# Folding a Fourier transform by residue, and moving the first output weights and the conv channel sums, in a hybrid trunk step

## What is computed

```python
hmix = rms_norm(x, norm_mix) * (1 + sc1) + sh1
q, k, v, conv_in, pool_in, four_in = split(hmix @ w_in)        # 2816 columns
attn = gqa_attention(rope(norm(q)), [cached keys, rope(norm(k))], ...)   # 8 heads of 64, 2 key heads
conv = silu(layer_norm(depthwise_conv31(a * sigmoid(gate))))   # 512 channels, norm over channels
pool = multi_scale_pool(pool_in) @ pool_w * pool_scale
four = fft2(four_in.reshape(L, 4, 128), axes=(0, 2)).real      # 4 groups, over tokens and channels
x = x + g1 * (concat([attn, conv, pool, four]) @ w_out)        # 2048 rows, 1024 columns
x = x + g2 * hier_moe(rms_norm(x) * (1 + sc2) + sh2)           # 16 experts, top 2 in one of 4 groups
y = rms_norm(x, final_norm)
```

## Time and profile before

| what | value |
|---|---|
| median of 3 runs (lowest, highest) | 703.83 us (702.86, 706.41) |
| the profiled execution: its own time | 707.6 us |
| its span, first to last instruction | 705.2 us |
| PE busy | 606.4 us (86%) |
| DVE busy | 532.2 us (75%) |
| ACT busy | 336.2 us (48%) |
| POOL busy | 140.2 us (20%) |
| mean granted TensorE clock | 0.944 |

### The profile page before, as it was taken

One profiled execution on the slowest core, in us unless ns is written; L12 is line 12 of the kernel. 1 busy time (PEld: TensorE's weight loads), 2 busy tenths in 40 slices (PEclk: granted clock), 3 DMA queues, 4 the chain that ended last, 5 costly groups with the idle time before them and its releaser, 6 DMA issues.

```text
span 705.2 us, 8279 instructions
## 1 busy us (share of the span) xinstructions
PE 606.4 (86%) x3212; PEld 483.0 (68%) x3212; DVE 532.2 (75%) x670; ACT 336.2 (48%) x446; POOL 140.2 (20%) x96
## 2 busy tenths in 40 slices
PE   0879999999999979999799999934999999999540
PEld 0269778899888656556578888824888887878430
DVE  0583599999999777998863520797999988888487
ACT  5143124331113645556645311363588887877542
POOL 0002000006994000000222432011132312221300
PEclk9989999999999989999999999975999999999865
DMA  7972955555002100000344400097799999997663
GB/s 274 413 266 97 348 179 179 185 201 207 12 2 86 59 0 1 1 0 1 120 145 164 150 1 1 0 363 300 266 381 396 387 362 362 379 350 281 225 275 149
DMA packets 44190, 133.44 MB, mean 189 GB/s; under 512 B 9328, under 2 KB 18132, under 8 KB 36472
## 3 DMA queue, kind: packets, MB, share of 16 engines
q1 hardware_dynamic: 36552, 121.49, 46.2%
q0 software_dynamic: 5184, 10.50, 3.9%
q10 hardware_dynamic: 2416, 0.92, 0.5%
HBM read 126.96 MB, written 14.32 MB: 200 GB/s over the span
## 4 chain that ended last, share of the span: by engine, by line
PE 47%; DVE 28%; DMA 17%; issue 3%; ACT 3%; SPq 1%; POOL 0%; ACTq 0%; DVEq 0%; POOLq 0%
DMA m_raw<-in_moe_w_down_dram 9%; DVE cy L1482 9%; PE ps L574 7%; PE ps L576 7%; PE ps L575 7%; DMA raw<-in_w_ada_dram 4%; PE ps L738 3%; PE ps L875 2%; PE ps L878 2%; PE ps L877 2%; DVE w_lo L1440 2%; PE ps L556 2%; DMA yb<-y_rows 1%; PE ps L865 1%; DVE ss_qk L1597 1%
## 5 line engine op out<-in xcount | busy, mean ns | idle before, releaser
L1482 DVE SCALAR_TENSOR_TENSOR cy<-cu,tapw,cy 128x655 f32<-128x655 f32 x120 | 114.7, 956 | 3.5
L1900 DVE TENSOR_TENSOR gu_lo<-m_raw,gu_hi 128x2048 fp32r<-128x2048 f32 x36 | 82.2, 2289 | 8.1 <-ACT gu_hi L1202 6.6
L1202 ACT ACTIVATE gu_hi<-m_raw 128x2048 fp32r<-128x2048 f32 x36 | 68.9, 1919 | 17.2 <-DMA m_raw<-in_moe_w_gate_dram 8.7
L875 PE MATMUL ps<-gu_hi,xt_h 128*128 128x512 f32 x144 | 60.3, 419 | 7.6 <-DVE gu_lo L1900 7.6
L1353 POOL TENSOR_TENSOR w_lo<-raw,w_hi 128x2048 fp32r<-128x2048 f32 x7 | 32.7, 4677 | 166.0 <-ACT w_hi L1130 166.0
L574 PE MATMUL ps<-w_hi,mix 128*128 128x512 f32 x160 | 62.9, 393 | 2.8 <-DVE w_lo L1679 2.8
L877 PEld LDWEIGHTS ps<-gu_lo,xt_h 128*128 128x128 f32 x288 | 56.3, 195 | 12.6
L576 PE MATMUL ps<-w_hi,mix 128*128 128x512 f32 x160 | 62.4, 390 | 0.0
L575 PE MATMUL ps<-w_lo,mix 128*128 128x512 f32 x160 | 62.3, 390 | 0.0
L878 PE MATMUL ps<-gu_hi,xt_l 128*128 128x512 f32 x144 | 58.5, 406 | 0.0
L877 PE MATMUL ps<-gu_lo,xt_h 128*128 128x256 f32 x288 | 58.4, 285 | 0.0
(11 more groups left out here) (351 smaller groups left out, 1426.7 us busy)
## 6 DMA issues: line engine op xcount, KB each, us to landing
raw<-in_w_ada_dram SPq DMA_DIRECT2D x24, 1024.0 KB, 7.5
m_raw<-in_moe_w_gate_dram SPq DMA_DIRECT2D x18, 1024.0 KB, 9.7
m_raw<-in_moe_w_up_dram SPq DMA_DIRECT2D x18, 1024.0 KB, 12.8
m_raw<-in_moe_w_down_dram SPq DMA_DIRECT2D x18, 1024.0 KB, 14.8
raw<-in_w_in_dram SPq DMA_DIRECT2D x11, 1024.0 KB, 7.1
raw<-in_w_out_dram SPq DMA_DIRECT2D x8, 1024.0 KB, 5.6
h_rows<-h2k SPq DMA_DIRECT2D x5, 512.0 KB, 12.0
ya<-y_rows SPq DMA_DIRECT2D x5, 512.0 KB, 7.6
```

The costliest lines, as they stand in the source:

```text
L875: pe.matmul(out, xt_h[q][:, k, :], gu_hi[q][:, k, :], start=(k == 0), stop=False)
L1202: act.activation(gu_hi[q][:, :, u * FF:(u + 1) * FF], m_raw[3 * s + u][:, :].rearrange("p (k n) -> p k n", k=KB), ACT.Copy).then_inc((g_hi ...
L1482: ins = dve.scalar_tensor_tensor(out=cy[:, blk, :], in0=cu[:, blk, i:i + CY], scalar=w, in1=cy[:, blk, :], op0=MUL, op1=ADD)
L1900: dve.tensor_tensor(gu_lo[s][u][:, :, :], m_raw[3 * s + u][:, :].rearrange("p (k n) -> p k n", k=KB), gu_hi[q][:, :, u * FF:(u + 1) * FF]. ...
```

## The change

1. **Fourier sums by residue.** DVE folds the four latent tiles (`fu0 - fu2`, `fu1 - fu3`, and the sum and the difference of the two sums) with six additions of 128 by 512. The table shrinks to 128 rows of 770 columns, and a head's eight latent products become four (256, 256, 128 and 128 columns, written to every second or fourth column of PSUM), one of two columns, and one of 256 for the context. The `fu` tiles are made in the order 0, 2, 1, 3, 4. `spectrum` still has five copies.
2. **Taps moved later.** Thirteen taps leave the stretch before the channel transform (`conv(8)`, `conv(6)`, `conv(6)` become 7 and 2, and two less among the keys); one each comes behind the first three channel products, one more in units 5 and 7, two in unit 8, and the last six stand behind the loop. The third block's additions to `csum` come in unit 1.
3. **First output weights early.** The high half of chunk 0 is copied in four pieces in units 4 to 7 into memory of its own, its low half is made on DVE in unit 8 in place of the raw weights.
4. **Channel sums behind chunk 0.** The sum of `csum` moves from ahead of chunk 0 to behind it, the sum of squares from ahead of chunk 1 into it (ahead of its fourth tile). Chunk 3 waits for the conv part block by block.
5. **GpSimd.** The low half of chunk 1 also waits for the last tap (`conv_made`).

```diff
-HN = N_LAT // 2 + 1
+HN = N_LAT // 2
+N_DFT = 6 * P + 2
+FU_ORDER = (0, 2, 1, 3, 4)
...
-            for t in range(LT):
-                chans = fu[:, t, h * P:(h + 1) * P]
-                pe.matmul(out[:, 0, 0:HN], chans, table[:, t, 0:HN], start=(t == 0), stop=(t == LT - 1))
-                pe.matmul(out[:, 1, 0:HN - 2], chans, table[:, t, HN:N_LAT], start=(t == 0), stop=(t == LT - 1))
...
+            for n, (made, dst, col, cols, first, last) in enumerate(((1, odd, 0, 2 * P, True, False), (2, odd, 2 * P, 2 * P, False, True),
+                                                                     (3, by4, 4 * P, P, True, True), (4, by4_2, 5 * P, P, True, True))):
+                if h == 0:
+                    pe.wait_ge(fold_made, made)
+                pe.matmul(dst, chans[n], table[:, col:col + cols].rearrange("p (a k) -> p a k", a=2), start=first, stop=last)
+            if h == 0:
+                pe.wait_ge(unit_out, N_UNITS)
+            pe.matmul(rest[:, 2 * P:2 * P + 2], chans[2], table[:, 6 * P:N_DFT], start=True, stop=True)
+            mm = pe.matmul(rest[:, 0:2 * P], chans[LT], cst[:, C_DPR:C_DPR + 2 * P], start=True, stop=True)
...
-        pe.wait_ge(ones_set, 1)
-        pe.wait_ge(conv_made, 4)
-        over_channels(pair(0, CY), csum).then_inc(sums_ps, 1)
...
-            if i == 1:
-                pe.wait_ge(csq_made, 5)
-                over_channels(pair(0, CY), csq[:, 0, :]).then_inc(sums_ps, 1)
...
-            if i == 3:
-                pe.wait_ge(cmix_lo, 4)
...
+                if i == 1 and t == 3:
+                    pe.wait_ge(csq_made, 5)
+                    over_channels(pair(0, CY), csq[:, 0, :]).then_inc(sums_ps, 1)
                 for kk in range(4):
+                    if i == 3 and t == 0:
+                        pe.wait_ge(cmix_lo, kk + 1)
...
+            if i == 0:
+                pe.wait_ge(ones_set, 1)
+                pe.wait_ge(conv_made, 4)
+                over_channels(pair(0, CY), csum).then_inc(sums_ps, 1)
...
+            ins = act.activation(wo_first[0][:, piece], raw[WO_SLOT[0]][:, piece], ACT.Copy)
...
+                if kt == 3 and 4 <= u < HEADS:
+                    first_wo_piece(u - 4)
...
-            if i >= 2:
+            if i >= 3:
...
-        wo_split(0)
         take_out(UNITS - 2)
...
                 pool.wait_ge(wo_lo, 1)
+                pool.wait_ge(conv_made, 4)
...
+        dve.tensor_tensor(fold[0][:, :], fu[:, 0, :], fu[:, 2, :], ADD)
+        dve.tensor_tensor(fu[:, 0, :], fu[:, 0, :], fu[:, 2, :], SUB).then_inc(fold_made, 1)
...
+            if u == HEADS:
+                conv(2)
+            if u == UNITS - 2:
+                dve.wait_ge(wo_hi, 1)
+                dve.tensor_tensor(wo_first[1][:, :], raw[WO_SLOT[0]][:, :], wo_first[0][:, :].bitcast(f32), SUB).then_inc(wo_lo, 1)
...
-            conv(min(len(taps), 4 if u in (1, 3) else 3))
-        dve.wait_ge(wo_hi, 1)
-        dve.wait_ge(pv_step, key_count(UNITS, 0))
-        dve.tensor_tensor(w_lo[0][:, :], raw[WO_SLOT[0]][:, :], w_hi[0][:, :].bitcast(f32), SUB).then_inc(wo_lo, 1)
+            if u < HEADS:
+                conv(4 if u % 2 else 3)
+        conv(len(taps))
         normal(3)
```

More of the change, by code:

```diff
@@ L425, in _ @@
             else:
[L426 removed]
+                sp.dma_start(raw[n % NRAW][:, 0:N_DFT], dft_d).then_inc(raw_in[n % NRAW], 16)
         sp.wait_ge(qk_made, 1)
@@ L652, in _ @@
                 pe.wait_ge(fpq_made, 1)
-            out = pair((1 + h) % 3, D).rearrange("p (a n) -> p a n", a=2)
-            for t in range(LT):
-                chans = fu[:, t, h * P:(h + 1) * P]
-                pe.matmul(out[:, 0, 0:HN], chans, table[:, t, 0:HN], start=(t == 0), stop=(t == LT - 1))
-                pe.matmul(out[:, 1, 0:HN - 2], chans, table[:, t, HN:N_LAT], start=(t == 0), stop=(t == LT - 1))
-            for part in range(2):
-                mm = pe.matmul(out[:, part, HN:HN + P], fu[:, LT, h * P:(h + 1) * P], cst[:, C_DPR + part * P:C_DPR + (part + 1) * P], start=True, stop=True)
+            lat, rest = latent_bank(h), rest_bank(h)
+            odd, by4, by4_2 = (lat.rearrange("p (a k s) -> p a k s", a=2, s=s)[:, :, :, o] for s, o in ((2, 1), (4, 0), (4, 2)))
+            chans = [fu[:, n, h * P:(h + 1) * P] for n in range(TT)]
+            for n, (made, dst, col, cols, first, last) in enumerate(((1, odd, 0, 2 * P, True, False), (2, odd, 2 * P, 2 * P, False, True),
[7 more added lines that the diff above has]
+            mm = pe.matmul(rest[:, 0:2 * P], chans[LT], cst[:, C_DPR:C_DPR + 2 * P], start=True, stop=True)
             mm.then_inc(fpq_ps, 1)
@@ L1581, in _ @@
             ins.then_inc(klo_made, 1)
-            conv(3 if kt in (1, 3) else 1)
+            conv(2 if kt in (1, 3) else 1)
         conv(2)
@@ L1645, in _ @@
                 queries_lo(h)
+                conv(1)
         dve.wait_ge(qs_hi, 4)
```

70 lines of the change are left out of this document (46 added, 24 removed).

## The result

The changed kernel takes 710.15 us (median of 22 runs, 705.95 to 711.74) against 707.07 (22 runs, 702.86 to 709.83) for the kernel before. The ratio is 1.0031, with a 95% interval of 1.0015 to 1.0046: 2 to 3 us slower (2.2 by the ratio, 3.1 by the medians). The profiled execution has a span of 707.2 us, against 705.2. By engine: PE 602.2 us, DVE 530.3, ACT 336.2, POOL 137.6, each within 4.2 us of before; the change is in the order, and busy shares don't show it.

What follows compares the result with a forecast made beforehand. It took a chain of waits through Fourier sums, attention (TensorE and VectorE alternating), conv norm and TensorE's output projection as the bound. Terms -6.5 + 1.4 + 7.7 = +2.6 us on 703.83 gave 706.4 us, range 700.8 to 711.0.

Steps and rivals of the forecast that it cites:

- the three signs that the prediction had named as showing it wrong: No TensorE wait between chunks 0 and 4; ScalarE's early Fourier list before 219; clock below 1.00 behind the new waits.
- Part 1: Fourier sums: channel transform starts 7.0 us earlier, less 0.5 us delay from taps behind channel products; gain 6.5 us.
- ScalarE still starts at 219.52: Fourier stretch: ScalarE's first key copy keeps its time, held 3.54 us by a GpSimd memset the change doesn't touch.
- upper bound of 8.4: Fourier sums: most the channel transform's start can gain, TensorE's work saved in four heads; lower bound 5 us.
- The strided PSUM writes: Fourier products written to every second or fourth column: cost between nothing and 5.4 us (doubling); taken as nothing.
- the rival of the unchanged pace: Fourier stretch: key handovers or strided writes set the pace, gain 3.5 instead of 6.5 us, 709.4 us; chance 0.13.
- Part 2: Attention: third block's two additions now fall in unit 1 on VectorE's chain, 1.4 us lost (0 to 1.7).
- Part 3: End of attention and output projection: chunk 0 starts 2.9 us earlier, but chunk 3 7.7 us late (4.7 to 10).
- new waits on GpSimd's low halves: Output projection: TensorE waits 2.8, 3.1 and 3.7 us before chunks 1, 2 and 3.
- Holds the first subtraction by about 2.0: Conv norm: GpSimd's work at 354.6 to 359.4 delays VectorE's first subtraction of the mean by about 2.0 us.
- The rival of the lower clock: TensorE's new waits drop its clock; seven us at the lower level cost 3.5 us, time 709.9; chance 0.20.

Runs made afterwards that it cites:

- taps_late: Kernel before, with the six taps beside GpSimd's last pooling steps moved to the end of the attention (units 8 and 9); 712.41 us, ratio 1.0086.
- fourier_gaps: Kernel before plus folded Fourier sums, old tail, ten displaced taps placed where VectorE waits, first channel-sum addition behind the keys; 699.35 us, ratio 0.9887.
- new_gaps: Changed kernel with taps placed as in fourier_gaps, none behind the attention, channel sum still behind chunk 0; 705.21 us, ratio 0.9967.
- clock_held: Changed kernel with TensorE's waits around the output chunks filled by matmuls the result doesn't use; 706.98 us, ratio 0.9992 to the kernel before.
- tail_only: Kernel before with the new tail alone (early first weights, moved sums, GpSimd's wait), old Fourier sums and tap places; 711.4 us, ratio 1.0070.
- fourier_only: Kernel before with the folded Fourier sums alone, old tail, the ten displaced taps run four to a unit in the attention; 710.31 us, ratio 1.0043.
- new_gaps_sum_first: new_gaps with the channel sum ahead of chunk 0 again, early first weights kept; ratio 0.9906 to the kernel before.
- second_sum_early: held_off with the sum of squares taken after one tile of chunk 1, not three; 696.44 us, ratio 0.9827 to the kernel before.
- held_off: new_gaps_sum_first with GpSimd starting chunk 1's low half only once the mean is subtracted from all four blocks; ratio 0.9909 to the kernel before.

## Why the prediction was right, and which of its steps failed

The forecast was 706.4 us, 2.6 more than before, in a range of 700.8 to 711.0; measured are 710.15 and 2.2 to 3.1 more, by ratio or by medians. Within the traces the terms were -6.5, +1.4 and +7.7; they measured -8.6, +3.0 and +9.8, together +4.3. All three signs were right and each size was too small. That the sum came so near to the measured difference is therefore luck in part: the gain was set 2.1 us too low, the two losses together 3.7 us. In the traces the difference is 4.3, in 22 executions of each kernel 2.2 to 3.1, so the terms hold for these two executions. Of the 3.7 us by which 706.4 lies under 710.15, 3.2 come from the start of the sum: 703.83 was a median of three, and 22 gave 707.07. Two of the three signs that the prediction had named as showing it wrong did appear: ScalarE's first key copy at 214.82, ahead of 219, and a clock below 1.00 behind a new wait.

- **Part 1.** The step that failed is "ScalarE still starts at 219.52", held by a memset that the change doesn't touch. The change moved the taps that slowed GpSimd in front of that memset. taps_late shows it alone: 1.7 us in a. With it the gain of 8.6 lies just over the upper bound of 8.4. The strided PSUM writes, priced between nothing and a doubling, cost nothing that shows, and the rival of the unchanged pace is out.
- **Part 2.** +1.4 for the additions in unit 1. fourier_gaps and new_gaps, with other places for taps and first addition, have 104.1 in b against 105.7, all three with the clock below 1.00 for some 12 us at the first scores: 1.6, about as predicted. The other 1.4 I put down to that low stretch, which was 8 us long in before's trace; clock_held, without one, has 102.7. No run tests that split by itself, but tail_only fits it: with before's taps in the attention and a low stretch of 12 us it has 104.4, 1.8 more than before.
- **Part 3, order.** Right: chunk 0 starts 0.94 us late (1.0 said), there are new waits on GpSimd's low halves before chunks 1, 2 and 3, and the mean comes 17.6 us behind the end of attention (350.68 - 333.11; 15 to 16 said).
- **Part 3, sizes.** The waits are 0.86, 2.60 and 3.49 (2.8, 3.1 and 3.7 said). Chunk 1's is small because chunk 0, at the low clock, ends some 1.7 us late (2 x 0.44 and 2 x 0.41 us lost in its two low windows). "Holds the first subtraction by about 2.0" failed: GpSimd was done at 346.88 + 4.56 = 351.44 and the subtractions began at 351.55, four in 3.09 us. From the mean to chunk 3's start it took 386.74 - 350.68 = 36.1, not 38.3. Counted from the last product with the values, chunk 3 starts after 54.8 us and not 47.6 (387.2 - 339.6): +7.2, near the 7.7, with two errors that nearly cancel (the mean 1.7 later than said, the chain 2.2 shorter). The rest of the 9.8 is chunk 3's first tile at the lower level, 5.6 us (392.33 - 386.74) where it took 2.95 (390.15 - 387.2).
- **The rival of the lower clock** came true in part, behind exactly the third, longest wait, at 2.6 us instead of 3.5, and, which no case had, at chunk 0, behind two waits of under a microsecond.

What no part of the prediction priced is what the displaced taps cost in front of the channel sum: some 6.5 us in d, in fourier_only and in taps_late alike. In the changed kernel they don't stand there. Its last tap is over at 337.19 + 5.49 = 342.68, and the sum waits for chunk 0 until 349.38; the taps delay the product into `cx` and with it chunk 1's halves, which the prediction had counted. The experiments price three of the changed kernel's places, the second and third with the earlier ones already mended: the places of the taps (new_gaps against the changed kernel, 4.5 to 4.9 us), the place of the first sum (new_gaps_sum_first against new_gaps, 4.7) and that of the second sum (second_sum_early against held_off, 4.8 by the medians).

## What to carry to other kernels

When a change takes work off one engine and puts some on another, follow the displaced work to where it lands: with ten taps in the waits of VectorE the folding gained 8.7 us, with six taps left behind the attention the same folding lost 2.9. A sum that starts a long chain belongs as early in its engine's order as its inputs allow, and after each repair the next link has to be looked up again: here the taps, the first sum and the second sum had to be moved in turn, and holding off GpSimd for the subtractions moved nothing while the second sum kept its place. Test a premise that another engine's time is fixed by looking at what runs beside it.
